# A hybrid attention and RWKV layer with experts: key norms inside block 4, pair 0 two steps earlier, head scores between turned weights and outputs

## The reference

```python
xn = rms_norm(h, g_mix)
proj = xn @ w_in                       # 2048 x 6144
dq, dk, dv, rr, rk, rv = split(proj)   # 1024 columns each
# group A: 8 heads of differential attention, causal, ALiBi
p = softmax(scores)                    # two score maps per head
a = p[0] - lam * p[1];  o = a @ v;  o = rms_norm(o) * (1 - lam_init)
# group B: 16 heads of RWKV-7, size 64
kk = k * k_k;  kk = kk / max(norm(kk), 1e-12)
state = state * w + (state @ -kk) b^T + v k^T;  y = state @ r
y = group_norm(y) * ln_w + ln_b + sum(r * k * r_k) * v;  y = y * g
h = h + concat(o, y) @ w_out
h = h + experts(rms_norm(h))           # top 1 of 4 groups, top 2 of 8 experts
```

## Time and profile before

| | us |
|---|---|
| median of 3 runs | 1617.46 |
| fastest, slowest run | 1616.53, 1619.32 |
| the profiled execution | 1620.23 |
| its span, from first to last instruction | 1618.3 |
| TensorE busy | 1354.6 |
| VectorE busy | 465.6 |
| ScalarE busy | 320.3 |
| POOL busy | 43.0 |

### The profile page before, as it was taken

The page is one execution under the profiler, slowest core; times in us unless marked ns, Lnnn a source line. Parts: engine busy times, 40 slices in busy tenths (PEclk is TensorE's granted clock), DMA queues, the critical chain, the costliest instruction groups (busy, mean ns, idle before and its releaser), DMA issues.

```text
span 1618.3 us, 22443 instructions
## 1 busy us (share of the span) xinstructions
PE 1354.6 (84%) x9350; PEld 720.4 (45%) x9350; DVE 465.6 (29%) x1086; ACT 320.3 (20%) x742; POOL 43.0 (3%) x91
## 2 busy tenths in 40 slices
PE   7999999999999989896966867867776877868765
PEld 6888878888887445431322222222222222222221
DVE  6032456676653551311101201201101101111003
ACT  2012122333322331121211211111111111111112
POOL 2000010000010000000000000000000000000000
PEclk9999999999999999898988978879878888888987
DMA  9433322222235329389999999999999999999994
GB/s 309 148 104 104 104 79 79 80 80 79 80 99 169 102 84 424 145 349 430 434 431 429 435 432 428 436 431 429 435 432 429 433 433 429 433 434 429 431 433 204
DMA packets 61910, 481.05 MB, mean 297 GB/s; under 512 B 8549, under 2 KB 27638, under 8 KB 48918
## 3 DMA queue, kind: packets, MB, share of 16 engines
q1 hardware_dynamic: 60962, 478.89, 72.6%
q10 hardware_dynamic: 884, 1.23, 0.2%
HBM read 478.01 MB, written 2.10 MB: 297 GB/s over the span
## 4 chain that ended last, share of the span: by engine, by line
PE 55%; DMA 38%; DVE 4%; ACT 1%; issue 1%; DVEq 0%; SPq 0%; POOL 0%; ACTq 0%
DMA ring<-in_moe_w_gate_dram 22%; DMA ring<-in_moe_w_up_dram 16%; PE ps L929 11%; PE ps L741 9%; PE ps L1155 8%; PE ps L1008 6%; PE ps L1174 3%; PE ps L1131 3%; PE ps L820 2%; PE ps L1182 2%; PE ps L1166 1%; PE ps L958 1%; PE ps L808 1%; PE ps L884 1%; PE ps L891 1%
## 5 line engine op out<-in xcount | busy, mean ns | idle before, releaser
L1155 PE MATMUL ps<-ring,oT 128*32 128x512 f32 x2048 | 337.8, 821 | 211.8 <-DMA ring<-in_moe_w_gate_dram 115.4
L1155 PEld LDWEIGHTS ps<-ring,oT 128*32 128x32 f32 x2048 | 83.1, 144 | 463.7 <-issue 310.1
L929 PE MATMUL ps<-xT,ring 128*128 128x256 f32 x768 | 190.7, 391 | 0.0
L2032 DVE TENSOR_TENSOR oT<-oT,ps 128x128 f32<-128x128 f32 x32 | 9.2, 288 | 592.8 <-ACT oT L1521 592.8
L929 PEld LDWEIGHTS ps<-xT,ring 128*128 128x128 f32 x768 | 138.6, 189 | 23.5 <-issue 3.6
L741 PE MATMUL ps<-xT,ring 128*128 128x256 f32 x640 | 139.4, 380 | 0.0
L741 PEld LDWEIGHTS ps<-xT,ring 128*128 128x128 f32 x640 | 121.2, 190 | 17.8 <-issue 1.5
L1174 PE MATMUL ps<-ring,oT 128*32 128x512 f32 x1024 | 119.4, 608 | 8.0 <-DVE oT L2032 7.9
L1008 PE MATMUL ps<-ring,oT 128*128 128x512 f32 x256 | 114.2, 597 | 1.9 <-DVE oT L1813 1.1
L1131 PE MATMUL ps<-xT,oT 128*32 128x512 f32 x512 | 115.3, 1030 | 0.0
L1166 PEld LDWEIGHTS ps<-fold,oT 128*128 128x128 f32 x512 | 59.6, 192 | 39.7 <-issue 39.7
(11 more groups left out here) (325 smaller groups left out, 1222.0 us busy)
## 6 DMA issues: line engine op xcount, KB each, us to landing
ring<-in_moe_w_gate_dram SPq DMA_DIRECT2D x32, 4096.0 KB, 32.5
ring<-in_moe_w_up_dram SPq DMA_DIRECT2D x32, 4096.0 KB, 33.3
ring<-in_moe_w_down_dram SPq DMA_DIRECT2D x31, 4096.0 KB, 32.5
ring<-in_w_in_dram SPq DMA_DIRECT2D x24, 1024.0 KB, 5.2
ring<-in_w_in_dram SPq DMA_DIRECT2D x32, 768.0 KB, 4.7
ring<-in_w_out_dram SPq DMA_DIRECT2D x16, 1024.0 KB, 5.2
ring<-in_moe_w_down_dram SPq DMA_DIRECT2D x2, 2048.0 KB, 30.8
res<-in_x_dram SPq DMA_DIRECT2D x2, 1024.0 KB, 6.7
```

What stands on the lines that cost most here:

```text
L929: last = mm(ps[:, 6 + (par + c) % 2, 0:S], wv[:, k, c * P:(c + 1) * P], xT[:, kq * KQ + k, :], start=(kq == 0 and k == 0), stop=(kq == 3 a ...
L1155: last = mm(ps[c * B:(c + 1) * B, 1 + j, :], xe[:, par, k, :], w[:, k, :], start=(kq == 0), stop=(kq == 3), tile_position=(0, c * B))
```

## The change

TensorE sums the key norms behind the first quarter of block 4. ScalarE takes the roots ahead of the copies of block 4, and those copies stand behind the exponentials of pairs 0 and 1. VectorE makes pair 1's plain factors and the unit keys of tiles 1 and 2 ahead of `mix_block(4)`, behind which a new semaphore `s_vmix` tells POOL that v may be staged. In block 5 pair 0's products come two steps earlier, the bonus too, and the inverse and `turn_vb` one step earlier; `turn_k` moves ahead of step 15. In the heads, `scores` and `attend` are each split in two: TensorE turns the weights, makes the scores of head h + 2, multiplies weights and values, and turns the values of head h + 2; VectorE makes the weights of head h directly behind the output of head h - 1, ahead of added tiles and of the maximum of head h + 1.

```diff
--- before.py
+++ after.py
@@ -267,6 +267,7 @@
         s_sq = sem("kk_squared")
         s_nrm = sem("kk_norms_summed")
         s_nst = sem("kk_norms_rooted")
+        s_vmix = sem("first_v_blocks_mixed")
 
         r_g = sem("pair_decay_summed")
         r_e = sem("pair_decay_exps")
@@ -657,7 +658,7 @@
                 g.tensor_scalar(at, at, col(V_LNB + n), None, ALU.add).then_inc(s_bg, 1)
 
             copy_factors(0, 0)
-            pool.wait_ge(r_g, 2)
+            pool.wait_ge(s_vmix, 1)
             g.tensor_copy(vst, projR[:, 2 * MT, :]).then_inc(r_vst, 1)
             cross_blocks(0, 0)
             shift_bonus(0)
@@ -721,6 +722,15 @@
                     last = turn(k, t)
             last.then_inc(s_xt, 1)
 
+
+            def key_sums():
+                pe.wait_ge(s_l3, 3 * MT)
+                for m in range(MT):
+                    if m % 2 == 0:
+                        pe.wait_ge(s_sq, m // 2 + 1)
+                    last = mm(ps[:, 4 + m // 2, (m % 2) * S:(m % 2 + 1) * S], same64[:, :], tmp[:, m, :], start=True, stop=True)
+                    if m % 2:
+                        last.then_inc(s_nrm, 1)
 
             def rkv_block(n, fold=False, outs=False):
                 for kq in range(4):
@@ -743,6 +753,8 @@
                         if kq == 3 and c < 3:
                             last.then_inc(s_pr, 1)
                     last.then_inc(s_free, 1)
+                    if outs and kq == 0:
+                        key_sums()
                     if fold and kq == 0:
                         pe.wait_ge(s_mask, 4)
                         pe.wait_ge(s_la, 4)
@@ -788,14 +800,6 @@
                     m, bank = 4 * half + i, 4 * (1 - half) + i
                     mm(ps[:, bank, 0:S], g2b[0:32, m * P:(m + 1) * P], tgb[0:32, :], start=False, stop=True).then_inc(s_l2, 1)
             rkv_block(4, outs=True)
-
-            pe.wait_ge(s_l3, 3 * MT)
-            for m in range(MT):
-                if m % 2 == 0:
-                    pe.wait_ge(s_sq, m // 2 + 1)
-                last = mm(ps[:, 4 + m // 2, (m % 2) * S:(m % 2 + 1) * S], same64[:, :], tmp[:, m, :], start=True, stop=True)
-                if m % 2:
-                    last.then_inc(s_nrm, 1)
             heads = [slice(0, L), slice(L, P)]
 
             def products(q, par):
@@ -937,15 +941,17 @@
             pe.sem_inc(r_y, 1)
             for i in range(16):
                 c, kq = i // 4, i % 4
-                if i == 4:
+                if i == 2:
                     pe.wait_ge(s_prA, 4 * RB)
                     products(0, 0)
-                elif i == 6:
+                elif i == 4:
                     bonus(0, 0)
-                elif 7 <= i < 15:
-                    inverse(0, i - 7)
+                elif 6 <= i < 14:
+                    inverse(0, i - 6)
+                elif i == 14:
+                    turn_vb(0, 0)
                 elif i == 15:
-                    turn_vb(0, 0)
+                    turn_k(0, 0)
                 if c == 0:
                     pe.wait_ge(s_ring[kq], (RB - 1) * 16 + 16)
                 if kq == 0:
@@ -961,7 +967,6 @@
                     last.then_inc(s_free, 1)
                 elif kq == 3:
                     last.then_inc(s_pr, 1)
-            turn_k(0, 0)
             pe.wait_ge(s_prA, 4 * RB + 3)
 
             def group_mean(m, bank, at):
@@ -1028,12 +1033,14 @@
                     rwkv_half(n, part)
                 done[0] = upto
 
-            def scores(h):
+            def turn_values(h):
                 if h > 1:
                     pe.wait_ge(t_ata, h - 1)
                 for t in range(TT):
                     last = pe.transpose(ps[:, 6, t * P:(t + 1) * P], projA[:, 2 * MT + h, t * P:(t + 1) * P], ident[:, :])
                 last.then_inc(t_vt, 1)
+
+            def scores(h):
                 if h > 1:
                     pe.wait_ge(t_mx, h - 1)
                 for c, rows in enumerate(heads):
@@ -1042,12 +1049,14 @@
                     mm(ps[:, bank, P:3 * P], projA[rows, h, P:2 * P], projA[rows, MT + h, :],
                        start=True, stop=True).then_inc(t_sc, 1)
 
-            def attend(h):
+            def turn_weights(h):
                 pe.wait_ge(t_a, h * 2 + 2)
                 pe.wait_ge(t_vta, min(h + 2, MT))
                 for n in range(3):
                     last = pe.transpose(ps[:, 6, n * P:(n + 1) * P], aw[:, n * P:(n + 1) * P], ident[:, :])
                 last.then_inc(t_at, 1)
+
+            def attend(h):
                 vtok = vtoks[h % 2]
                 if h:
                     pe.wait_ge(t_ov, h)
@@ -1062,16 +1071,22 @@
             pe.wait_ge(s_paA, 3 * MT + 3)
             pe.wait_ge(s_vo, MT - 1)
             scores(0)
+            turn_values(0)
             rwkv_halves(1)
             group_variance(MT - 1, 3, 0)
             rwkv_halves(2)
             pe.wait_ge(s_vo, MT)
             scores(1)
+            pe.wait_ge(t_vta, 1)
+            turn_values(1)
             for h in range(MT):
                 rwkv_halves(HALVES[h])
+                turn_weights(h)
+                if h + 2 < MT:
+                    scores(h + 2)
                 attend(h)
                 if h + 2 < MT:
-                    scores(h + 2)
+                    turn_values(h + 2)
             rwkv_halves(2 * MT)
             pe.wait_ge(s_on, TT)
             for m in range(MT):
@@ -1313,7 +1328,6 @@
                 for i in range(4):
                     act.wait_ge(s_l2, 12 * half + (MT + i + 1))
                     a.copy(gate[:, 4 * half + i, :], ps[:, 4 * (1 - half) + i, 0:S]).then_inc(s_l3, 1)
-            rkv_copies(4)
             for b in range(4):
                 act.wait_ge(s_nrm, b + 1)
                 a.activation(tmp[:, 2 * b:2 * b + 2, :], ps[:, 4 + b, :].rearrange("p (a b) -> p a b", a=2),
@@ -1363,10 +1377,11 @@
             act.sem_inc(r_yw, 1)
             exps(0)
             state_scales(0)
+            act.wait_ge(r_prep, 1)
+            exps(1)
+            state_scales(1)
+            rkv_copies(4)
             last_block_copy(0)
-            exps(1)
-            act.wait_ge(r_g, 2)
-            state_scales(1)
             power(0, 0)
             last_block_copy(1)
             power(0, 1)
@@ -1771,23 +1786,25 @@
             decay_sums(0, first=True)
             plain_factors(0, 0)
             decayed_factors(0, 0, first=True)
+            key_norms(1)
+            unit_keys(1)
+            decay_sums(1)
+            plain_factors(1, 1)
+            key_norms(2)
+            unit_keys(2)
             mix_block(4)
+            own.join()
+            dve.sem_inc(s_vmix, 1)
             mask_products(0, 0)
             triangles(0, 0)
-            decay_sums(1)
             bonus(0, 0)
             power(0, 0)
-            key_norms(1)
             power(0, 1)
-            unit_keys(1)
-            plain_factors(1, 1)
             power(0, 2)
             inverse_step(0, 2)
             decayed_factors(1, 1)
             inverse_step(0, 3)
             whole_inverse(0, 0)
-            key_norms(2)
-            unit_keys(2)
 
             def centre(m, bank, at):
                 dve.wait_ge(s_mean, m + 1)
@@ -1928,15 +1945,15 @@
             variance(MT - 1, 3, 0)
             group_factors(MT - 1)
             group_output(MT - 1)
+            head_weights(0)
             head_max(1)
-            head_weights(0)
             for h in range(1, MT + 1):
                 head_output(h - 1)
+                if h < MT:
+                    head_weights(h)
                 add_tiles(HALVES[h - 1] // 2)
                 if h + 1 < MT:
                     head_max(h + 1)
-                if h < MT:
-                    head_weights(h)
             dve.wait_ge(s_sst, 1)
             own.mark(v.reciprocal(rst, rst))
             own.join()
```

## The result

| | before | after |
|---|---|---|
| median, us | 1617.32 (1616.53 to 1619.32, 4 runs) | 1625.78 (1624.99 to 1629.65, 4 runs) |
| ratio to before | | 1.0055 (0.95 interval 1.0042 to 1.0067) |
| profiled execution, us | 1620.23 | 1629.65 |
| its span, us | 1618.3 | 1627.7 |

The change costs 8.5 us. The forecast was 1617.0 and "within". The profiled execution of after is its slowest of four, and this matters here, because what costs the time does not fall out alike in every execution. Only the profiled execution of a kernel has a trace: what the others did is known by their times alone.

A forecast was written before the change was run, and what follows sets the result against it. TensorE's work before the expert weight stream at 698 us was taken to set the end. Block terms of -1.2 and head terms of +0.7 gave -0.5 us, so a median of 1617.0 us, range 1614.3 to 1619.5.

The forecast's parts named there:

- within: Whole kernel: time change no larger than about 0.2% (3.2 us), not distinguishable from no change; chance 0.79.
- What bounds the kernel: Expert weight stream fills DMA from 698 us; TensorE's gains or losses before that move the end by as much.
- Part 1: Key sums, pair 0 and block 5: old waits go, two new ones come, sum -1.2 us.
- waits of 0.3, 1.9 and 1.0 us: Block 5, TensorE's waits for VectorE ahead of the bonus and inverse steps 0 and 3: predicted to go.
- (a): Block 5: ScalarE's copy of tile 1 holds up its power copy; new 1.7 us wait ahead of inverse step 2.
- (b): End of block 5: token_k copied behind tile 3, so the first solve's wait grows from 0.9 to 1.2 us.
- Part 2, the chain: Heads 2, 4, 6: turned-weights copy waits behind exps, output copies 8.4 us apart instead of 7.44; +2.9 us.
- Part 2, head 1: Heads 1, 3, 5: two half tiles, 7 us, cover the dependent work and the wait goes; -2.1 us.
- The rival of the clock: Heads 2, 4, 6: new waits of 2.2, 2.2, 3.1 us lower the clock; 7 us more, 1624 us; chance 0.06.

The follow-up runs named there:

- mended kernel: Kernel with only the block 4, block 5 and pair 0 changes, plus ScalarE copying tile 1 after the second power and token k before tile 3: 1611.10 us.
- half-filled kernel: Changed kernel with two or three unread products added in each of TensorE's new waits in heads 1, 2, 4 and 6: 1619.76 us.
- filled kernel: Changed kernel with four to seven unread products added in each of TensorE's new waits in heads 1, 2, 4 and 6: 1616.59 us.
- block part: Changed kernel with the heads put back as before, so only block 4, block 5 and pair 0 are changed: 1613.98 us, ratio 0.9985 to before.
- heads alone: Kernel before with only the heads changed: 1625.84 us, ratio 1.0063 to before.
- exps behind the copy: Changed kernel with ScalarE copying head h's turned weights before making the exps of head h+1: 1612.19 us.
- VectorE's old order: Changed kernel with VectorE's order in the heads as before (next head's maximum ahead of the weights), TensorE's new order kept: 1614.27 us.
- router's wait filled: Kernel before with eleven unread products put into TensorE's 5.3 us wait for the router: 1617.19 us, ratio 1.0002 to before.

## Why the prediction was wrong, step by step

**What bounds the kernel**: right. The loss of 8.7 us at the end of the heads (616 us) is 9.1 at the load behind the first read and 9.4 in the span.

**Part 1**: right in each step of the trace. The waits of 0.3, 1.9 and 1.0 us went; (a) is 1.88 us (forecast 1.7), (b) 1.15 (1.2); the sum is -1.3 against -1.2, and the mended kernel shows that both came from ScalarE's order. The medians say -2.9, with an interval from -1.1 to -3.9 that holds -1.3. If there is a rest, it may be the slow stretch behind the router, which ended early in that kernel's profile; one trace of each kernel does not show it for the medians.

**Part 2, the chain**: right. 8.38 us against 8.4; waits of 2.6, 2.6 and 3.5 us in heads 2, 4 and 6 against 2.2, 2.2 and 3.1, so TensorE's own work between two attends was 0.4 us less than I had put, for the distance is as forecast.

**Part 2, head 1**: the first step that failed. I wrote that in heads 1, 3 and 5 "two half tiles, 7 us, cover the chain and the wait goes". I had followed the weights to attend, and not the tile that VectorE adds behind them to the bank which the next half tile wants. head_weights was moved ahead of add_tiles as well as of head_max, and only the second was worked out. It costs 2.6 us, and in the profiled execution 1.7 more by the fall of the clock behind it.

**The rival of the clock**: the step that decided. The sum put the clock in the short heads at nothing. The mechanism of the rival, its place and its size (7 us) are what the runs show: 7.7 us in the heads of the profiled executions, 6.0 of them behind the three waits that it named and 1.7 behind that of head 1, and 9.2 on the medians. What failed is its chance. I took 2.2 us to be nearer to the harmless 1.9 than to the 5.3 of the router and gave 0.06. The waits were longer than I had worked out and there were four of them, and 2.2 us is enough (the half-filled kernel). A range of 1614.3 to 1619.5 had no place for it, though the zone that no row of mine covered, between 1.9 and 5.3 us, held all of the forecast's new waits in the heads. The Trainium skill's page "TensorE: Matmul & The Clock Gate", section "HAM oscillation — how this bites in real kernels", describes how waits between short groups of matmuls make each group start slowly; the trace of after agrees with it, with 8.83 instead of 7.13 us behind 2.61 us of waiting, and the filled kernel shows it by taking it away. The waits in that section's example are some 3 to 5 us; here the clock fell behind 2.2 to 3.5 us, and the measurement decides. So the page, by its example, would not have settled the waits of 2.2 us either.

**Waits alone**: 1616.59 us with the clock taken out of it. The forecast of 1617.0 without a fall of the clock is near this, but by luck, for two errors cancel: the missed wait of head 1, +2.6, and the block part, 1.7 us better on the medians than its sum, a difference within its interval.

## What to carry to other kernels

Before a step is moved in a list written by hand, write down for every engine what stands ahead of it and behind it there, and for each of these the buffer that it frees: both new waits of block 5, the three of the short heads and the one of head 1 are things that nobody had moved. A new wait of TensorE that is longer than those which rows show to be harmless is to be costed twice, once as itself and once with the work behind it at half clock; with several such waits, the second cost deserves more than a small chance. Filling a wait with products that nobody reads can show in one run whether the clock is the cause, and whether a wait is worth removing for its own sake, if the trace of the filled kernel is read for the clock too: behind the router it fell in spite of the filling.

## What the runs showed of the hardware

A wait of 2.2 us (waits half filled, head 6) to 3.5 us between groups of matmuls can be followed by a granted clock at its lower level, 1.2 GHz, and the work behind it then takes 1.5 to 2.9 us more. It need not be: of four waits of 2.6 to 3.5 us, one was followed by a fall in the profiled execution of the heads alone, all four in that of after, though at different distances, and one of 2.82 us by none in the kernel with exps behind the copy. Waits of 0.9, 1.2, 1.6 and 1.9 us around block 5 and in the heads were followed by none in any trace here. The spread of the executions was 1.8 us with the waits filled and 11.1 with them open (heads alone), but it is no sure sign: VectorE's old order, with no wait above 1.5 us in the heads, had 7.4, and the kernel before, in the same group, 6.4. Behind the logits the clock was 0.73 from 675 to 680 us with TensorE busy 5.00 of 5 us, in the kernel before with the router's wait filled, so filling a wait does not always hold it; why it fell there is left open.
